# Order of the three partial products of a weight block in a two-block transformer kernel

## What is computed

```python
h = layer_norm(DEEPNORM_ALPHA * h + 0.5 * swiglu(h, ffa_w_in[i], ffa_w_out[i]), ...)
mix = hybrid_mixer(h, ...)      # gated delta rule, stick-breaking attention, latent attention
h = layer_norm(DEEPNORM_ALPHA * h + mix, ...)
h = layer_norm(DEEPNORM_ALPHA * h + 0.5 * swiglu(h, ffb_w_in[i], ffb_w_out[i]), ...)
h = h + sigmoid(h @ ple_w_gate[i]) * (p[i] @ ple_w_proj[i])
```

## Time and profile before

| | |
|---|---|
| median of three runs | 3495.43 us |
| span of the profiled execution, first to last instruction | 3490.0 us |
| the profiled execution's own device time | not listed; the median lies 5.43 us above the span |
| TensorE matmul busy | 3305.1 us, 95% of the span |
| VectorE busy | 2335.2 us, 67% |
| ScalarE busy | 1581.0 us, 45% |
| GpSimd busy | 483.0 us, 14% |
| mean granted TensorE clock | 0.976 |
| matmuls of `multiply` (lines 252, 253 and 254) | 2184 of each |

### The profile page before, as it was taken

How to read it: one execution, slowest core, us unless ns; L and a number is a source line. 1 busy time by engine, 2 the same in 40 slices (tenths; PEclk the granted TensorE clock), 3 DMA queues, 4 the chain that set the end, 5 groups by cost and what they waited for, 6 DMA issues and landing times. The chain is left out here.

```text
span 3490.0 us, 59574 instructions
## 1 busy us (share of the span) xinstructions
PE 3305.1 (95%) x24514; PEld 2821.9 (81%) x24514; DVE 2335.2 (67%) x3196; ACT 1581.0 (45%) x2553; POOL 483.0 (14%) x399
## 2 busy tenths in 40 slices
PE   8999998899999999999998899999999989989998
PEld 8998775778998699986767689986899856669986
DVE  7877475548875488764845488755887258758852
ACT  5552435236552355524352365524655254645541
POOL 0003113540003000031135300030000100300001
PEclk9999999999999999999999999999999999999999
DMA  4235220012235223452200123342333222122331
GB/s 159 100 132 189 74 67 32 4 50 97 98 133 167 75 105 103 136 178 74 67 26 4 50 97 109 134 157 74 127 109 112 82 68 73 43 85 86 109 108 61
DMA packets 81590, 327.38 MB, mean 94 GB/s; under 512 B 11905, under 2 KB 11905, under 8 KB 65833
## 3 DMA queue, kind: packets, MB, share of 16 engines
q1 hardware_dynamic: 81320, 323.57, 27.4%
HBM read 321.15 MB, written 4.74 MB: 93 GB/s over the span
## 5 line engine op out<-in xcount | busy, mean ns | idle before, releaser
L236 DVE TENSOR_TENSOR w_low<-w_raw,w_high 128x1024 fp32r<-128x1024 f32 (+1 forms) x241 | 340.1, 1412 | 441.4 <-ACT w_high L228 440.5
L228 ACT ACTIVATE w_high<-w_raw 128x1024 fp32r<-128x1024 f32 (+1 forms) x241 | 284.6, 1183 | 526.6 <-PE ffa_ps L254 170.6
L834 DVE TENSOR_TENSOR w_low<-w_raw,w_high 128x1024 fp32r<-128x1024 f32 (+1 forms) x186 | 220.9, 1188 | 21.4 <-ACT w_high L713 10.7
L713 ACT ACTIVATE w_high<-w_raw 128x1024 fp32r<-128x1024 f32 (+1 forms) x186 | 190.3, 1023 | 3.0 <-PE ffa_ps L254 1.6
L252 PE MATMUL mix_proj_ps<-mix_x_high,w_high 128*128 128x512 f32 x416 | 169.7, 408 | 13.1 <-DVE mix_x_low L401 13.0
L254 PE MATMUL mix_proj_ps<-mix_x_high,w_low 128*128 128x512 f32 x416 | 166.5, 400 | 0.0
L253 PE MATMUL mix_proj_ps<-mix_x_low,w_high 128*128 128x512 f32 x416 | 165.5, 398 | 0.0
L252 PE MATMUL ffa_ps<-ffa_hid_high,w_high 128*128 128x512 f32 x352 | 141.4, 402 | 0.5 <-DVE w_low L236 0.5
L252 PE MATMUL b_f_ps<-b_f_hid_high,w_high 128*128 128x512 f32 x352 | 139.6, 397 | 0.5 <-DVE w_low L236 0.5
L253 PE MATMUL b_f_ps<-b_f_hid_low,w_high 128*128 128x512 f32 x352 | 139.2, 396 | 0.0
L254 PE MATMUL b_f_ps<-b_f_hid_high,w_low 128*128 128x512 f32 x352 | 139.2, 395 | 0.0
(11 more groups left out here) (748 smaller groups left out, 10942.2 us busy)
## 6 DMA issues: line engine op xcount, KB each, us to landing
ffa_quarters<-in_ffa_seven SPq DMA_DIRECT2D x40, 1024.0 KB, 4.8
ffb_quarters<-in_ffb_seven SPq DMA_DIRECT2D x40, 1024.0 KB, 4.8
b_f_quarters<-in_ffn_seven SPq DMA_DIRECT2D x40, 1024.0 KB, 5.0
w_raw<-in_mix_in SPq DMA_DIRECT2D x77, 512.0 KB, 3.4
w_raw<-in_ffa_out SPq DMA_DIRECT2D x32, 704.0 KB, 5.7
w_raw<-in_ffb_out SPq DMA_DIRECT2D x32, 704.0 KB, 5.4
w_raw<-in_ffn_out SPq DMA_DIRECT2D x32, 704.0 KB, 4.1
ffa_ada_raw<-in_w_ada SPq DMA_DIRECT2D x80, 256.0 KB, 2.9
```

What stands on the lines that cost most here:

```text
L228: act.activation(self.high[:, self.place(n, 0, kt)], self.raw[:, n % SLOTS, :kt * P], ACT.Copy).then_inc(self.rounded, 1)
L236: dve.tensor_tensor(self.low[:, whole], self.raw[:, n % SLOTS, :kt * P], self.high[:, whole].bitcast(F32), ALU.subtract).then_inc(self.spl ...
L713: act.activation(ops.split(group, r)[0], ops.source(group, r), ACT.Copy).then_inc(part_rounded, 1)
L834: dve.tensor_tensor(low, ops.source(group, r), high.bitcast(F32), ALU.subtract).then_inc(part_split, 1)
```

## The change

The call waits for the rounding of its block first, multiplies all chunks of the call by the high weights (two matmuls each), then waits for the split and multiplies all chunks by the low weights.

```diff
         places = range(kt) if part is None else part
-        pe.wait_ge(self.split, g + 1)
+        pe.wait_ge(self.rounded, g + 1)
         for place in places:
             k = order[place]
             if ready is not None:
                 pe.wait_ge(ready, k0 + place + 1)
-            w_high, w_low = (w[:, self.place(g, k)] for w in (self.high, self.low))
+            w_high = self.high[:, self.place(g, k)]
             pe.matmul(out, w_high, x_high[:, k0 + k, :], start=start and place == 0, stop=False)
             pe.matmul(out, w_high, x_low[:, k0 + k, :], start=False, stop=False)
-            mm = pe.matmul(out, w_low, x_high[:, k0 + k, :], start=False, stop=stop and place == kt - 1)
+        pe.wait_ge(self.split, g + 1)
+        for place in places:
+            k = order[place]
+            mm = pe.matmul(out, self.low[:, self.place(g, k)], x_high[:, k0 + k, :], start=False,
+                           stop=stop and place == kt - 1)
```

## The result

| | before | after |
|---|---|---|
| median | 3495.49 us (5 runs, 3493.58 to 3502.16) | 3513.76 us (5 runs, 3509.22 to 3514.64) |
| ratio | | 1.0048, 95% interval 1.0037 to 1.0060 |
| span of the profiled execution | 3490.0 us | 3512.8 us |
| mean granted TensorE clock | 0.976 | 0.974 |

The changed kernel is slower by 16.8 us by the ratio (13 to 21), 18.3 by the medians. The forecast was +6.5 us with a range that ended at 3509. The five runs of before here include the three named at the start.

A forecast was written before the change was run, and what follows sets the result against it. TensorE, busy 95% of the span, was taken to bound the kernel. 9.0 + 3.0 - 5.5 = +6.5 us on the 3490.0 span gave 3496.5, plus 5.43 to the median: 3501.9 us, range 3496 to 3509.

The forecast's parts named there:

- Cost 1: First out block of each of six feed-forwards: low products run behind the last hid_low chunk, 1.5 us each, +9.0 us.
- The gains: Waits for w_low vanish at the fourth blocks of both ple and both ffb: -5.5 us, bounds 1.8 and 5.9.
- The guess on the clock: Second ple's fourth block: with only 1.0 us of wait left, the clock stays up, another 1.6 us gained.
- the pair of rows: Granted clock behind ple's waits: 0.84 in the second ple, 1.00 in the first with its wait of 1.35 us.
- Cost 2: Openings of stages: low products run behind the waits for chunk 1 or 2, +3.0 us, bounds 1.6 and 6.0.
- b_mo: Opening of this output projection, where two chunk waits bind: a loss of 0.6 us is kept.
- 2 us for where the half-clock stretches fall: Allowance in the forecast's own range of 3498 to 3506, beside the bounds of its terms.
- a later wait that swallows theirs: Both mix_out openings: a later wait takes up the delay, so no loss is kept there.
- The out blocks' loss: Rival, chance 0.1: the 9.0 us of the feed-forwards vanish into a later wait, 3492.9 us.
- A met wait in the middle of a block: Rival, chance 0.05: this wait isn't free in each of 393 calls; 0.11 us each gives 3545 us, 0.05 gives 3521.
- The change did what it says: Rival that the change does less, w_low being nearly always ready: the forecast's own ground, within 0.1% without Cost 1.

The follow-up runs named there:

- openings alone: Kernel before, with low products deferred only in the calls by parts, in the 14 openings: 3508.70 us, ratio 1.0034.
- filled version: Kernel before, low products deferred only in eleven first parts of multiply_first, plus 22 useless matmuls in the pauses between chunks: 3497.63 us, ratio 1.0015.
- whole blocks alone: Kernel before, with new order and rounding wait only in whole-block calls that wait for nothing but their weights: 3490.36 us, ratio 0.9984.

## Why the prediction was wrong, point by point

- **Cost 1, the first out blocks: right.** The second block was forecast to start 1.58 us later and to give 0.08 back, 1.5 us each; in the trace it is 1.51 to 1.53 and 1.43 to 1.45, with the waits for hid_low and the low products in a row as described. By an estimate from the gap that the Trainium skill ("TensorE: Matmul & The Clock Gate", Back-to-back issue gap) gives, the term was 7.7 us; the trace has 8.6, with the eleven low products at 0.233 us each (245.57 to 248.13).
- **The gains: right.** 5.4 us in the trace where 5.5 was forecast, 3.65 of them in the second ple, including the clock that stays up. The guess on the clock went by the pair of rows. It held, and on average its size did too (1.6 us), but with some luck: one kernel kept the whole wait and its full clock. More than half of these gains come with the wait for the rounding, and not with the order.
- **Cost 2, the openings: this is the step that failed.** It said: "Kept are 0.4 and 0.2 (ffa), 0.4 (first mix_proj), 0.5 three times (both b_f, b_proj), and 0.6 in b_mo", 3.0 us with an upper bound of 6.0. (The items listed add up to 3.1.) The openings alone cost 11.9 us (7.7 to 16.4). Two things were left out of the working.
- *First, the clock was taken as given.* I moved matmuls along the timeline of before and kept its stretches at half clock in place, with "2 us for where the half-clock stretches fall". At the opening of the last feed-forward the low parts of the activations come every 1.4 us, and three products at half clock take 1.3: TensorE had next to no pause. Two take 0.86, and the pause that comes with them keeps the granted clock down (0.50 instead of 0.79 over 8 us), so that the delayed products and the second block run at half clock as well. The filled version shows this: more matmuls, 4.9 us faster, and the half-clock stretch back to 4.6 us from 8.0. The 0.43 us were there in the earlier trace rows, but the 1.4 us were not: the three arrivals in those rows are 0.60 us apart, and those of the last feed-forward stood in the trace, but in no row that I picked. Both b_f and b_proj lost 1.3 to 2.4 us in the changed kernel, where 0.5 each was forecast.
- *Second, the arrivals were taken as given.* "Both mix_out have a later wait that swallows theirs" was wrong: the wait that was to swallow the loss moved with it. It ends for a chunk that hangs on the sums of line 1090, and these stand in TensorE's own list behind the low products. From the second pair to the end of that wait it is 3.94 us in both kernels, and 3.94 as well in the version with only the output projections' openings changed. (The 5.7 us in the expectation above are counted to the last chunk, one later.) With both pairs in front of the low products the wait is gone and the two mix_out lose 2.2 us together instead of 4.0. The two steps meet here: a longer half-clock stretch with the old order delays the sums, and the opening with them, by 0.9 us. How the rest divides between the late sums and the low products themselves isn't settled.
- **The rivals.** The out blocks' loss wasn't given back. A met wait in the middle of a block costs nothing that can be seen: whole blocks alone, with such a wait in 186 of the 393 calls, are faster than before, and at 0.05 us each they would lose 9 us. The change did what it says. That openings lose by the clock was no rival of mine, and the range ended 5 us short. Even with every term at its own worst bound (9.6 + 6.0 - 1.8) the sum would be 3509.2 us, so it is the openings' bound that failed, and not the choice of the range.
- **b_mo: right.** 0.6 us, in every version that defers there. Both ffb and both ple openings swallow what they lose, as forecast, but for 0.5 us in the second ffb and 0.9 in the first ple in the changed kernel; the first ple shows up to 0.5 with its old order too.

## What to carry to other kernels

In this kernel, reordering an accumulation so that the late operand comes last paid at most where the call waits for nothing else, and there waiting later, in the old order, gave most of it. Behind waits for single chunks, the products taken out of the gaps are run after the last arrival. Where a wait seems to swallow a delay, follow its releaser back: if that hangs on an instruction in the same engine's list behind the moved work, the wait moves too. At a cold opening ask for each arrival whether TensorE still has enough to do at half clock until the next one comes.

## What was unexpected

- Two pauses, of 0.28 and 0.44 us by the distance of the starts, in the first 3 us of an opening went with a clock that stayed at its lower level: 0.50 against 0.79 over 8 us, with TensorE shown as busy for 7.67 of them. It was so in all three traces with that order, and in none of the ten without the pauses. The busy share hides it, since it counts a matmul at half clock as busy for 0.63 us; the distance of the starts shows it.
- 22 matmuls whose result is thrown away made a kernel faster, 3502.48 to 3497.63 us by the medians of 11 runs each (3.5 us by the means).
- Two waits of 0.82 and 1.31 us with 0.7 us of matmuls between them left the clock up in the one trace that has them, where one of 2.93 brought it down in seven traces of eight. So the granted clock has some chance in it, and a gain by it has to be read from more than one trace.
